# Turning the rotary part of the queries with four DMAs in place of a product with a permutation, and the order of the groups in a quarter

## What is computed

```python
cq = rmsnorm_2(u @ w_dq, q_lora_norm)
q = jnp.einsum('bsr,rhd->bshd', cq, w_uq)
q_nope = q[..., :QK_NOPE_DIM]
q_rope = apply_rope(q[..., QK_NOPE_DIM:], cos, sin)
# apply_rope(x): x1, x2 = the two halves of the 64 columns
#   concatenate([x1 * c - x2 * s, x1 * s + x2 * c])
s = (einsum('bqhd,bkhd->bhqk', qn_b, k_nope) + einsum('bqhr,bkr->bhqk', qr_b, k_rope)) * scale
p = softmax(where(key_pos <= q_pos, s, -inf));  o = einsum('bhqk,bkhd->bqhd', p, v)
```

## Time and profile before

| | |
|---|---|
| median of 3 runs | 2398.97 us (2398.51 to 2399.20) |
| the profiled execution | 2398.69 us, its span 2396.7 us |
| PE busy | 2334.8 us, 97% of the span |
| DVE, ACT, POOL busy | 1671.9, 1005.2, 888.4 us |
| granted PE clock over the span | 0.991 |

### The profile page before, as it was taken

How to read it: one execution, slowest core, us unless ns; L and a number is a source line. 1 busy time by engine, 2 the same in 40 slices (tenths; PEclk the granted TensorE clock), 3 DMA queues, 4 the chain that set the end, 5 groups by cost and what they waited for, 6 DMA issues and landing times. The chain is left out here.

```text
span 2396.7 us, 33477 instructions
## 1 busy us (share of the span) xinstructions
PE 2334.8 (97%) x13500; PEld 2022.0 (84%) x13500; DVE 1671.9 (70%) x1627; ACT 1005.2 (42%) x1259; POOL 888.4 (37%) x461
## 2 busy tenths in 40 slices
PE   7999889999989999999999999999999999999998
PEld 5889677788869999989999979999967778799997
DVE  5688578774279696768786768786777743596874
ACT  4323343432254353454353454353443342443443
POOL 1220322121147355437454336454321101383551
PEclk8999999999999999999999999999999999999999
DMA  4222222222313333223333233323320113223322
GB/s 146 79 71 71 70 71 97 95 88 97 96 62 115 106 106 106 89 71 108 121 94 100 88 106 98 123 94 101 106 58 22 35 53 105 88 86 109 124 84 84
DMA packets 217695, 217.14 MB, mean 91 GB/s; under 512 B 10593, under 2 KB 215008, under 8 KB 217568
## 3 DMA queue, kind: packets, MB, share of 16 engines
q1 hardware_dynamic: 217024, 215.14, 28.4%
q10 hardware_dynamic: 544, 0.20, 0.0%
HBM read 213.22 MB, written 2.10 MB: 90 GB/s over the span
## 5 line engine op out<-in xcount | busy, mean ns | idle before, releaser
L1234 PE MATMUL bank<-Xhi,wlo 128*128 128x256 f32 x1152 | 321.3, 279 | 0.0
L1235 PE MATMUL bank<-Xlo,whi 128*128 128x256 f32 x1152 | 321.2, 279 | 0.0
L1236 PE MATMUL bank<-Xhi,whi 128*128 128x256 f32 x1152 | 321.2, 279 | 0.0
L631 POOL TENSOR_TENSOR sums<-raw 128x512 f32<-128x512 f32 x72 | 144.1, 2001 | 429.8 <-DMA raw<-in_ffn_post_wg_dram 161.6
L933 ACT ACTIVATE whi<-raw 128x2048 fp32r<-128x2048 f32 x72 | 138.2, 1920 | 370.4 <-PE bank L1242 242.0
L1240 PE MATMUL bank<-xghi,wlo 128*128 128x512 f32 x624 | 248.9, 399 | 28.0 <-DVE xglo L1874 22.2
L746 ACT ACTIVATE whi<-raw 128x2048 fp32r<-128x2048 f32 x74 | 141.2, 1907 | 249.9 <-PE bank L1242 235.9
L1242 PE MATMUL bank<-xghi,whi 128*128 128x512 f32 x624 | 245.1, 393 | 0.0
L1863 DVE TENSOR_TENSOR wlo<-raw,whi 128x2048 fp32r<-128x2048 f32 x57 | 131.7, 2310 | 160.3 <-ACT whi L746 160.1
L1234 PE MATMUL bank<-Xhi,sxlo 128*128 128x256 f32 x864 | 242.1, 280 | 0.3
L1236 PE MATMUL bank<-Xhi,sxhi 128*128 128x256 f32 x864 | 240.9, 279 | 0.0
(11 more groups left out here) (356 smaller groups left out, 6077.5 us busy)
## 6 DMA issues: line engine op xcount, KB each, us to landing
raw<-in_ffn_w_up_dram SPq DMA_DIRECT2D x22, 1024.0 KB, 5.1
raw<-in_ffn_pre_wg_dram SPq DMA_DIRECT2D x22, 1024.0 KB, 5.3
raw<-in_ffn_pre_wu_dram SPq DMA_DIRECT2D x22, 1024.0 KB, 5.3
raw<-in_ffn_post_wg_dram SPq DMA_DIRECT2D x22, 1024.0 KB, 5.4
raw<-in_ffn_post_wu_dram SPq DMA_DIRECT2D x22, 1024.0 KB, 5.4
raw<-in_ffn_pre_wd_dram SPq DMA_DIRECT2D x24, 768.0 KB, 4.4
raw<-in_ffn_post_wd_dram SPq DMA_DIRECT2D x24, 768.0 KB, 4.4
raw<-in_w_in_dram SPq DMA_DIRECT2D x14, 1024.0 KB, 5.0
```

What stands on the lines that cost most here:

```text
L631: nc.gpsimd.tensor_tensor(s1, a21, a22, ALU.add).then_inc(adds_done[h], 1)
L1234: nc.tensor.matmul(bank, wl, x, start=first, stop=False, skip_group_check=True)
L1235: nc.tensor.matmul(bank, w, xl, start=False, stop=False, skip_group_check=True)
L1236: return nc.tensor.matmul(bank, w, x, start=False, stop=last, skip_group_check=True)
```

## The change

The two products with the permutation go. In each quarter ACT issues four DMAs in their place (`turn_queries`): each copies 32 partitions of 1024 columns (128 KB) of `QRr` to the 32 partitions beside them in `QRs`, a part of `work`. A DMA copies without a sign, so the first 32 rows of the sines of each 64 are negated once, ahead of the stage (`sin_signed`). The product with the sines then reads `QRs` in SBUF where it read a PSUM bank. The order of the groups changes too: rotary queries first (groups 4 and 5), then values (6 to 9), then the queries of heads 0 to 3 (10 to 13), so a quarter has 14 groups where it had 16. All waits on counts follow.

```diff
@@ ACT
+            def turn_queries(q):
+                a.wait_ge(evacuated, q * 14 + (GB["attn"] + 6))
+                for b in range(4):
+                    src, dst = slice(b * 32, b * 32 + 32), slice((b ^ 1) * 32, (b ^ 1) * 32 + 32)
+                    nc.scalar.dma_start(QRs[dst, :], QRr[src, :]).then_inc(qrope_turned, 16)
...
                 if isinstance(q, int):
-                    split_hi(UB["w_o"] + 1, 1, groups_done, q * 16 + (GB["attn"] + 10))
-                    split_hi(UB["w_o"], 0, groups_done, q * 16 + (GB["attn"] + 16))
+                    turn_queries(q)
+                    split_hi(UB["w_o"] + 1, 1, groups_done, q * 14 + (GB["attn"] + 6))
+                    split_hi(UB["w_o"], 0, groups_done, q * 14 + (GB["attn"] + 14))
                 else:
-                    rope_hi(q * 2 + (UB["attn"] + 3), q + 1, q * 16 + (GB["attn"] + 10))
-                    a.wait_ge(groups_done, q * 16 + (GB["attn"] + 16))
+                    turn_queries(q)
+                    rope_hi(q * 2 + (UB["attn"] + 3), q + 1, q * 14 + (GB["attn"] + 6))
+                    a.wait_ge(groups_done, q * 14 + (GB["attn"] + 14))
                     keys_hi(q * 2 + (UB["attn"] + 2), q + 1, 0, UNIT, 4)
@@ PE
-                for j in range(2):
-                    bank = group(12 + j)
-                    pe.wait_ge(evacuated, q * 16 + (gb + 9 + j))
-                    nc.tensor.matmul(bank, perm[:, :], tile(QRr, j), start=True, stop=True
-                                     ).then_inc(groups_done, 1)
@@ DVE
+            for b in (0, 2):
+                minus = rope_q[b * 32:b * 32 + 32, T:2 * T]
+                nc.vector.tensor_scalar(minus, minus, -1.0, None, ALU.mult).then_inc(sin_signed, 1)
...
                 for j in range(2):
                     take(10 + j, tile(QN, j))
+                v.wait_ge(qrope_turned, q * 64 + 64)
+                v.wait_ge(sin_signed, 2)
                 for j in range(2):
-                    v.wait_ge(groups_done, q * 16 + (gb + 13 + j))
-                    v.wait_ge(qrope_part, q * 2 + (j + 1))
-                    nc.vector.tensor_tensor(tile(QRr, j), banks[4 + j][:, :], rope_q[:, T:2 * T], ALU.mult
-                                            ).then_inc(evacuated, 1)
-                    v.wait_ge(evacuated, q * 16 + (gb + 13 + j))
-                    nc.vector.tensor_tensor(tile(QRt, j), tile(QRt, j), tile(QRr, j), ALU.add
+                    nc.vector.tensor_tensor(tile(QRs, j), tile(QRs, j), rope_q[:, T:2 * T], ALU.mult
+                                            ).then_inc(qrope_part, 1)
+                for j in range(2):
+                    v.wait_ge(qrope_part, q * 4 + (j + 3))
+                    nc.vector.tensor_tensor(tile(QRt, j), tile(QRt, j), tile(QRs, j), ALU.add
                                             ).then_inc(qrope_ready, 1)
```

More of the change, by code:

```diff
@@ L50 @@
           ("ffn1", 38, 0), ("pool", 2, 0), ("ffn2", 38, 0), ("kv", 2, 4), ("ffn3", 38, 0), ("dq", 2, 4),
-          ("attn", 8, 64), ("w_o", 8, 8), ("ffn4", 38, 0), ("x_out", 0, 8)]
+          ("attn", 8, 56), ("w_o", 8, 8), ("ffn4", 38, 0), ("x_out", 0, 8)]
 UB, GB = {}, {}
@@ L259, in build @@
         QRr = Prb[:, 0:2 * T]
+        QRs = work[:, 2 * T:4 * T]
         def probs(h):
@@ L288, in build @@
         keys_split = sem("keys_split")
+        qrope_turned = sem("qrope_turned")
+        sin_signed = sem("sin_signed")
         raw_ready = [sem("raw_ready0"), sem("raw_ready1")]
@@ L1736, in group @@
                 def group(n):
-                    pe.wait_ge(evacuated, q * 16 + (gb + n - 7))
+                    if n == 7:
+                        pe.wait_ge(small_log, 7)
+                        pe.wait_ge(outlo_ready, q * 4 + 1)
+                    if n > 7:
+                        pe.wait_ge(evacuated, q * 14 + (gb + n - 7))
                     return banks[n % 8][:, :]
@@ L1747, in queries @@
                     m.then_inc(groups_done, 1)
[L1749 to L1756, removed]
                 unit_ready(q * 2 + (UB["attn"] + 1), 1)
@@ L1759, in attend @@
                 for j in range(2):
-                    bank = group(8 + j)
+                    bank = group(4 + j)
                     for kt in range(QR):
@@ L1765, in attend @@
                     m.then_inc(groups_done, 1)
-                queries(0, 10)
-                queries(1, 11)
-                for j in range(2):
-                    bank = group(12 + j)
-                    pe.wait_ge(evacuated, q * 16 + (gb + 9 + j))
-                    nc.tensor.matmul(bank, perm[:, :], tile(QRr, j), start=True, stop=True
-                                     ).then_inc(groups_done, 1)
-                queries(2, 14)
-                queries(3, 15)
+                unit_ready(q * 2 + UB["attn"], 0)
+                for x in range(4):
+                    c = slice(x * P, (x + 1) * P)
+                    three(group(6 + x), ckhi[:, c], cklo[:, c], w0[0][:, 512:1024], w0[1][:, 512:1024],
+                          True, True).then_inc(groups_done, 1)
+                for x in range(4):
+                    queries(x, 10 + x)
                 def scores(h, i0=0, i1=TC):
@@ L1812, in attend @@
                     if h == 0:
-                        pe.wait_ge(evacuated, q * 16 + (gb + 16))
+                        pe.wait_ge(evacuated, q * 14 + (gb + 14))
                     for i in range(TC):
@@ L2483, in take, with take_values @@
                 def take(n, dst):
-                    v.wait_ge(groups_done, q * 16 + (gb + n + 1))
+                    v.wait_ge(groups_done, q * 14 + (gb + n + 1))
                     nc.vector.tensor_tensor(dst, banks[n % 8][:, :], R[:, :], ALU.mult).then_inc(evacuated, 1)
-                for n in range(4, 8):
-                    v.wait_ge(groups_done, q * 16 + (gb + n + 1))
-                    nc.vector.tensor_copy(tile(VV, n % 4), banks[n][:, :]).then_inc(evacuated, 1)
+                def take_values(n):
+                    v.wait_ge(groups_done, q * 14 + (gb + n + 1))
+                    nc.vector.tensor_copy(tile(VV, n - 6), banks[n % 8][:, :]).then_inc(evacuated, 1)
@@ L2490, in attend @@
                 v.wait_ge(small_root, 7)
                 for j in range(2):
-                    take(8 + j, tile(QRr, j))
+                    take(4 + j, tile(QRr, j))
+                take_values(6)
+                take_values(7)
                 for j in range(2):
-                    v.wait_ge(evacuated, q * 16 + (gb + 9 + j))
+                    v.wait_ge(evacuated, q * 14 + (gb + 5 + j))
                     nc.vector.tensor_tensor(tile(QRt, j), tile(QRr, j), rope_q[:, 0:T], ALU.mult
@@ L2506, in attend @@
                                             ).then_inc(qrope_ready, 1)
                 for j in range(2):
-                    take(14 + j, tile(QN, 2 + j))
+                    take(12 + j, tile(QN, 2 + j))
                 def maxes(h, i0=0, i1=TC):
```

8 lines of the change are left out of this document (5 added, 3 removed).

## The result

The changed kernel takes 2401.81 us (median; 2400.88 to 2404.34) against 2398.60 beside it (2397.23 to 2400.94): a ratio of 1.0014, with an interval of 1.0008 to 1.0020. It is slower by 3.2 us, where 2396.7 had been forecast in a range of 2393.8 to 2400.8. With 20 executions of each kernel the interval is +1.9 to +4.8 us, so the loss is told from none, small as it is. The miss is 5.1 us, and its sign is wrong. The profiled execution took 2401.77 us, its span is 2400.0 us, and its granted clock is 0.989 where it was 0.991.

The account below looks back on a forecast made before the run. PE was taken to bound the kernel, busy 97% of the span. A gain of 5.1 us in quarters 0 to 2 and a loss of 2.8 in quarter 3 gave -2.3 on 2398.97: 2396.7 us, range 2393.8 to 2400.8.

Parts of the forecast that it names:

- The stretched row of DVE: Quarter 3 before the change: a sum with both inputs in SBUF lasts 2.99 us under POOL's 4.60 us subtraction.
- The row that was to show that PSUM reads aren't held (1818.37): Quarter 1 before the change: two DVE operations reading PSUM take 1.27 us, the usual 0.6 each, so no stretching.
- quarters 0 to 2: Loop quarters: scores at t = 11.06 instead of 12.77, a gain of 1.7 us each, -5.1 us for three.
- the copies are hidden: Loop quarters: the four copies land near t = 8.3, before DVE needs them at 9.10, so no wait.
- Rival (e): Copies land late in each loop pass; each us beyond t = 9.1 costs 1 us in three quarters; chance 0.15.
- 0.43 each: ACT's four DMA issues in each quarter: 0.43 us apiece, the last issued at t = 5.1, ACT free at 5.52.
- rival (b): Quarter 3: the first sum loses the race to POOL's second subtraction, scores 5.3 us late, 2399.2 us; chance 0.20.
- (c): Quarter 3: issues take 0.3 us each, both sums pass, +0.4 to +0.9 there, 2394.3 to 2394.8 us; chance 0.15.
- the likeliest case: Quarter 3: first sum passes, second waits for POOL's second subtraction, +2.8 us there, 2396.7 us in all; chance 0.40.

Follow-up runs that it names:

- the wait is filled: Changed kernel with 34 unused products on PE in quarter 3, between the last queries and the first scores: 2400.26 us, ratio 1.0004.
- Two ahead: Changed kernel, in quarter 3 with two of the four DMA issues before ACT's first split of `w_o` and two behind it: 2395.49 us, ratio 0.9990.
- one ahead: Changed kernel, in quarter 3 with one DMA issue before ACT's first split of `w_o` and three behind it: 2392.62 us, ratio 0.9979.
- three ahead: Changed kernel, in quarter 3 with three DMA issues before ACT's first split of `w_o` and one behind it: 2400.56 us, ratio 1.0013.
- second cut short: Changed kernel with POOL's second subtraction of quarter 3 on 64 of its 2048 columns, the first one whole: 2397.65 us, ratio 0.9996.
- copies in the old order: Changed kernel with the old order of groups, values before rotary queries, the four copies issued once those are out: 2413.57 us, ratio 1.0056.

## Why the prediction was wrong

**Right: where it is decided.** It named quarter 3, the two products with the sines and the two sums on DVE, and POOL's two subtractions of `w_o`. The stretched row of DVE showed the mechanism before the change. The row that was to show that PSUM reads aren't held (1818.37) proves nothing, as it starts after POOL's subtraction had ended at 1817.90. But another one of the kernel before does, inside POOL's 1912.44 to 1917.04:

```profile
1913.88 0.69 DVE L2502 TENSOR_TENSOR Prb<-bank,rope_q 128x512 f32<-128x512 f32 x1 [0.17 <-PE bank L1771]
```

**Right within 0.15: quarters 0 to 2.** Forecast were scores at t = 11.06 and 1.7 us a quarter; measured are 11.11 and 1.55. The scores do come 1.66 earlier, but 0.11 is lost again before the transposes (7.74 from scores to transposes, where it was 7.63 in quarter 1). The products with the sines, forecast for t = 9.10, start at 9.09. POOL's subtraction in the loop (t = 7.29 to 8.59 in quarter 2) stays clear of them.

**Right: the copies are hidden.** Forecast was a landing near t = 8.3. One line's instructions, L1155, with the time from issue to landing:

```profile
L1155 ACTq DMA_DIRECT2D work<-Prb x16: 518/612/949, 1764.8 to 1904.2; - x16
...
DMA to landing us min/median/max: 2.2/2.3/2.7
```

In quarter 3 the last is issued at t = 5.61 (1904.2) and lands at 8.08, in quarters 1 and 2 at 7.9, and nothing waits for them. Rival (e) is out. The estimate from the Trainium skill ("SBUF — State Buffer", "Door 1: The DMA port swizzle") of 2.8 us for four such copies is close to 2.2 to 2.7, but these are times of single copies behind one another, so no run here measures that bandwidth. From the first issue to the last landing it is 4.3 us, 2.45 of them the issues.

**Wrong: the term "0.43 each" for the four issues.** This is the step that failed. They take 0.61 each, and ACT's next instruction starts another 0.42 later, which the sum had put at nothing. Instead of 5.52, ACT starts the first split at t = 6.64 (0.03 less for the first issue's start, 0.73 more for the four, 0.42 for the step behind them), and POOL runs from 8.70 to 13.27 where 7.58 to 12.18 had been worked out. POOL's second subtraction started at t = 13.34, to the hundredth as forecast. So of DVE's four operations not three were through by then but one. The text had put the point from which rival (b) decides at "0.1 us more in the four issues"; it was 1.12 more, past (b), in a case that no rival priced. The rows taken for 0.43 were those of issues of another kind, small loads from DRAM, while the copies have 32 partitions of 1024 columns at both ends. They were also two of seventeen: the prediction says that ACT's issues at the kernel's start are 0.44 to 0.47 apart, but in that same view they take from 0.28 to 0.58. The two ends, from ACT's queue in the kernel before:

```profile
1.20 0.58 ACTq L735 DMA_DIRECT2D rows<-in_pre_mix_g_dram  x1
1.81 0.28 ACTq L735 DMA_DIRECT2D rows<-in_post_mix_g_dram  x1
```

So the cost should have been carried through from 0.28 to 0.58: (c) took 0.3 each, but nothing took 0.6.

**Missing: the clock.** No step asked what PE's idling does to its speed afterwards. It cost 2.47 us: 2.47 more between scores and transposes, gone when the wait is filled. PE works for 5.06 us at half its speed, which makes 2.53. The Trainium skill ("TensorE: Matmul & The Clock Gate", Part 1) says that the clock has two levels and that PE falls to the lower one when it idles; the traces agree, with 0.50 at the end of 8.2 us of waiting and 1.00 when the wait is filled.

**The rest of the working was right.** Two ahead sets POOL's first subtraction to t = 7.11, before the forecast's 7.58, and gives just the course of the likeliest case: the first sum passes, the second is held, the first maximum comes at t = 19.51 (forecast 19.5), quarter 3 loses 2.86 us (forecast 2.8), and the time is 2.3 below the kernel before (forecast 2.3). That the last two agree is in part luck: its loop quarters gain 4.65 and not 5.1, the four quarters together are 1.82 shorter, and the other 0.5 lies within the 1 us by which the time outside the stage varies from one execution to another.

So with the true start of POOL (8.70 to 13.27) the same steps give, for the change: the first product starts at 13.13, the second comes at 13.74, behind POOL's 13.34, and is held to 17.7; the first sum ends at 19.0, scores at 19.1. Measured is 19.37, as POOL's second subtraction took 4.82 and not 4.51. Without the clock that is +6.0, with the 2.47 of the clock +8.4; less 4.65 is +3.8. The four quarters show +4.1 and the medians +3.2.

What stays open: why ACT starts its split 0.42 after the fourth issue, and only 0.13 after the last where one, two or three issues stand ahead of it; why the clock falls behind one short wait and not behind another (below); and how the medians' +3.2 divides beyond the stage.

## What to carry to other kernels

When a change turns a PSUM read of DVE into a second SBUF read, list what POOL reads from SBUF at that time in every quarter or pass, not only in the loop, and move POOL's work behind DVE's, here by moving two splits in ACT's program: that turned +3.2 us into -7.8. When a forecast hangs on which of two engines is first, work it out again with the uncertain cost at twice its value: 0.65 us in POOL's start decided over 5 us. A wait of PE can cost more than its own length, since a slower clock can follow it.

## What the runs showed of the hardware

- **Who is next.** The Trainium skill ("SBUF — State Buffer", "Who interferes with whom") says that the engine that issues first has the shared pair for its whole instruction; all rows here agree (0.7 of work took 4.72 and 4.98 us under POOL's 4.57 and 4.82). The order of the recorded starts decides even where both have work waiting. Against POOL's second subtraction at t = 13.33 or 13.34, DVE's operations recorded from 12.78, 12.79 (one and two ahead) and 9.10 went first, and those from 13.39, 13.42 and 13.74 (two ahead, three ahead, the change) were held for the whole of it. So two subtractions ready back to back let just one waiting DVE operation in between: its follower is recorded 0.4 behind POOL's second. That second is recorded at 4.82 instead of about 4.5, so part of it seems to be a wait for the product.
- **An issue has a length of its own kind.** 0.61 us for a copy of 32x1024 from SBUF to SBUF (0.52 to 0.95), 0.28 to 0.58 for the small loads at the kernel's start. The fourth issue cost more than its length: with it behind the split, POOL starts 0.94 earlier (8.70 to 7.76), and with each further one 0.65 and 0.63. While ACT is already computing, its queue goes on issuing. Three ahead, the timelines of ACT and its queue:

```profile
1905.15 1.92 ACT L749 ACTIVATE whi<-raw 128x2048 fp32r<-128x2048 f32 x1 [4.72 <-DVE VV L2500]
1905.46 0.52 ACTq L1155 DMA_DIRECT2D work<-Prb  x1
```

- **The clock after a wait.** In these stretches the granted clock is at 1.00 or at 0.50 and nothing between; a mean of 0.72 or 0.53 only says for how much of its stretch it was low. The loss between scores and transposes is about half the time that PE works at the lower level, which is the price of working at half the speed:

| quarter | PE waits | works at the lower level | transposes later than 7.74 after the scores |
|---|---|---|---|
| 3, the change | 8.20 | 5.1 | 2.47 |
| 3, three ahead | 7.29 | 3.1 | 1.51 |
| 3, second cut short | 4.03 | 3.1 | 1.47 |
| 3, copies in the old order | 10.85 | 3.8 | 1.86 |
| 1, copies in the old order | 2.02 | 3.4 | 1.69 |
| 2, copies in the old order | 2.02 | 0 | 0 |
| 3, two ahead | 2.36 | 3.4 | hidden |
| 3, one ahead | 1.74 | 0 | 0 |

A longer wait isn't followed by a slower stretch in step, and the same wait of 2.02 us was followed by one in quarter 1 and by none in quarter 2. In that quarter 1 and with two ahead, the clock fell about 1 us after PE had taken up its work again. The two-ahead case, busy time from the scores on:

```profile
1913.05:1918.55 5.50, 5.50 (x17) 3.47 (x18) 5.50 (x3) 0.00 (x0) 4.31 (x1) 0.69 0.00 0
```

There it cost next to nothing: quarter 3 lost 2.86 us where 2.8 had been worked out without it. The clock was back by t = 17.84, and DVE was held by POOL until 18.38.
